# One 64-wide product in place of two 32-wide ones in the 96-row items of a mixture-of-experts kernel

## The reference

```python
def swiglu(x, w13, w2):
    g, u = jnp.split(x @ w13, 2, axis=-1)
    return (jax.nn.silu(g) * u) @ w2

for e in range(N_EXPERTS):          # 8 experts, D_MODEL 1024, D_FF_EXPERT 3584
    out = out + gates[:, e:e + 1] * swiglu(xt, w13[e], w2[e])
```

## Time and profile before

| what | value |
|---|---|
| time, median of 3 runs | 1376.26 us (1376.21 to 1376.49) |
| the profiled execution | 1376.58 us, its span 1374.7 us |
| granted TensorE clock, mean | 0.996 |
| TensorE busy | 1347.6 us, 98% of the span |
| bytes moved by DMA | 444.58 MB |

### The profile page before, as it was taken

The page is one execution under the profiler, slowest core; times in us unless marked ns, Lnnn a source line. Parts: engine busy times, 40 slices in busy tenths (PEclk is TensorE's granted clock), DMA queues, the critical chain, the costliest instruction groups (busy, mean ns, idle before and its releaser), DMA issues.

```text
span 1374.7 us, 29896 instructions
## 1 busy us (share of the span) xinstructions
PE 1347.6 (98%) x13281; PEld 1063.0 (77%) x13281; DVE 411.8 (30%) x761; ACT 321.8 (23%) x587; POOL 13.9 (1%) x27
## 2 busy tenths in 40 slices
PE   9999999999999999999999999999999999999994
PEld 6989888888798888888557888557888557887542
DVE  6677555554747753200100100100100100100102
ACT  6445454443644533000001000001000000000001
POOL 1000000000000000000000000000000000000000
PEclk9999999999999999999999999999999999999998
DMA  8826345555543569999999999999999999999992
GB/s 317 314 96 223 124 169 184 184 187 190 191 154 123 185 250 399 413 378 352 409 421 420 420 419 419 420 421 419 420 420 420 420 421 420 420 420 420 421 420 116
DMA packets 63901, 444.58 MB, mean 323 GB/s; under 512 B 7262, under 2 KB 8686, under 8 KB 10905
## 3 DMA queue, kind: packets, MB, share of 16 engines
q1 hardware_dynamic: 61976, 437.22, 79.7%
q0 software_dynamic: 1792, 5.41, 1.1%
HBM read 441.16 MB, written 1.44 MB: 322 GB/s over the span
## 4 chain that ended last, share of the span: by engine, by line
PE 93%; DVE 3%; DMA 2%; issue 1%; ACT 1%; SPq 0%; DVEq 0%; ACTq 0%
PE bank L1860 52%; PE bank L1440 10%; PE bank L1442 10%; PE bank L1441 10%; PE bank L1824 2%; DMA slot_yT_hi<-in_moe_units 2%; PE bank L1922 2%; PE bank L1834 1%; PE bank L1528 1%; PE bank L1482 1%; PE bank L1835 1%; DVE w_lo L826 1%; PE bank L1649 1%; PE bank L1569 1%; PE bank L1632 1%
## 5 line engine op out<-in xcount | busy, mean ns | idle before, releaser
L1373 DVE TENSOR_TENSOR hidden<-hidden,bank 128x384 f32<-128x384 f32 (+1 forms) x56 | 27.3, 487 | 587.7 <-ACT hidden L786 587.7
L826 DVE TENSOR_TENSOR w_lo<-raw,w_hi 128x1024 fp32r<-128x1024 f32 x154 | 181.1, 1219 | 42.8 <-ACT w_hi L524 41.3
L524 ACT ACTIVATE w_hi<-raw 128x1024 fp32r<-128x1024 f32 x154 | 154.5, 1057 | 40.5 <-PE bank L1442 40.5
L786 ACT ACTIVATE hidden<-bank 128x384 f32<-128x384 f32 (+1 forms) x56 | 24.5, 437 | 365.5 <-PE bank L1860 365.5
L1860 PE MATMUL bank<-raw,mid_x 128*32 128x384 f32 (+1 forms) x1632 | 92.8, 380 | 1.0 <-ACT mid_x L760 1.0
L1860 PEld LDWEIGHTS bank<-raw,mid_x 128*32 128x32 f32 x1632 | 88.7, 110 | 4.5 <-issue 3.1
L779 ACT ACTIVATE hT<-bank 128x384 f32<-128x384 f32 (+1 forms) x56 | 24.5, 437 | 288.5 <-PE bank L1922 288.5
L1440 PE MATMUL bank<-xT_hi,w_hi 128*128 128x256 f32 x320 | 91.8, 287 | 0.0
L1441 PE MATMUL bank<-xT_lo,w_hi 128*128 128x256 f32 x320 | 90.5, 283 | 0.0
L1442 PE MATMUL bank<-xT_hi,w_lo 128*128 128x256 f32 x320 | 90.4, 283 | 0.0
L1440 PE MATMUL bank<-w_hi,xT_hi 128*128 128x512 f32 (+1 forms) x224 | 85.2, 380 | 1.1 <-DVE w_lo L826 0.6
(11 more groups left out here) (326 smaller groups left out, 2100.1 us busy)
## 6 DMA issues: line engine op xcount, KB each, us to landing
raw<-in_moe_units SPq DMA_DIRECT2D x102, 1024.0 KB, 24.9
slot_w_hi<-in_moe_units SPq DMA_DIRECT2D x51, 1024.0 KB, 25.8
slot_w_lo<-in_moe_units SPq DMA_DIRECT2D x51, 1024.0 KB, 26.0
raw<-in_layer_units SPq DMA_DIRECT2D x44, 1024.0 KB, 5.1
raw<-in_dense_units SPq DMA_DIRECT2D x33, 1024.0 KB, 4.9
slot_bias<-in_moe_units SPq DMA_DIRECT2D x17, 1024.0 KB, 26.0
slot_qk<-in_moe_units SPq DMA_DIRECT2D x17, 1024.0 KB, 26.4
slot_memT_lo<-in_moe_units SPq DMA_DIRECT2D x17, 1024.0 KB, 26.7
```

The source lines that it names most:

```text
L524: act.activation(w_hi[:, st.split(u), half, :], raw[:, st.slot(u), half * n:(half + 1) * n], ACT.Copy)\
L786: act.activation(hidden[:, 0:n * P], bank[2][:, 0:n * P], ACT.Silu).then_inc(sem("silu"), 1)
L826: dve.tensor_tensor(w_lo[:, st.split(u), half, :], raw[:, st.slot(u), half * n:(half + 1) * n], w_hi[:, st.split(u), half, :].bitcast(F32) ...
L1373: dve.tensor_tensor(hidden[:, 0:n * P], hidden[:, 0:n * P], bank[j % 2][:, 0:n * P], ALU.mult)\
```

## The change

In the 96-row items tokens 0 to 63 become one product with 64 stationary columns, where they were two products with 32. In `mid_up` that is the case for every k-block, in `mid_down` for blocks 0, 1 and 2, in both banks; block 3 stays as it was. Tokens 64 to 95 (group 2) and everything in group 3 keep 32 columns. The results of each output element are the same sums as before.

```diff
         def mid_up(w, k, b, start, stop):
             a = (k % 4) * 512
-            for g in range(3):
-                r = slice(g * 32, (g + 1) * 32)
+            for r in (slice(0, 64), slice(64, 96)):
                 product(bank[b][r, 0:384], mid_x[:, k, r], w[:, a:a + 384], start, stop)
             for g in range(3):
                 mm = product(bank[b][96:128, g * P:(g + 1) * P], mid_x[:, k, g * 32:(g + 1) * 32], w[:, a + 384:a + 512],
...
             def group(g):
                 return rows[:, block, g * 32:(g + 1) * 32] if block < 3 else rows[:, g, 96:128]
 
-            for g in range(3):
-                product(bank[4][g * 32:(g + 1) * 32, :], group(g), w[:, a:a + 512], start, stop)
+            first_two = ((slice(0, 64), rows[:, block, 0:64]),) if block < 3 else \
+                tuple((slice(g * 32, (g + 1) * 32), group(g)) for g in range(2))
+            for r, held in first_two:
+                product(bank[4][r, :], held, w[:, a:a + 512], start, stop)
+            product(bank[4][64:96, :], group(2), w[:, a:a + 512], start, stop)
             for g in range(2):
                 product(bank[4][96:128, g * 256:(g + 1) * 256], group(g), w[:, a + 768:a + 1024], start and g == 0, stop)
-            for g in range(3):
-                product(bank[5][g * 32:(g + 1) * 32, 0:256], group(g), w[:, a + 512:a + 768], start, stop)
+            for r, held in first_two:
+                product(bank[5][r, 0:256], held, w[:, a + 512:a + 768], start, stop)
+            product(bank[5][64:96, 0:256], group(2), w[:, a + 512:a + 768], start, stop)
             return product(bank[5][96:128, 0:256], group(2), w[:, a + 768:a + 1024], start, stop)
```

## The result

The changed kernel takes 1921.97 us (median of 4 runs, 1921.69 to 1922.43) against 1376.24 us for the kernel before on the same chip: a ratio of 1.3965 (95% interval 1.3941 to 1.399), 545.7 us more. The forecast was 1932 us, in a range of 1760 to 2040.

What follows compares the result with a forecast made beforehand. The prediction took 96-row items as bound by TensorE and 64-row items as living on the weight ring. Adding +410 (k-blocks), +153 (down halves) and -7 (waits) gave +556 us, so 1932 us, range 1760 to 2040.

Steps and rivals of the forecast that it cites:

- part 1: In 96-row items, removing one product per k-block and two per changed down half is worth nothing; the fourth group sets the pace.
- part 2: Inside 96-row items, each change between 64-wide and 32-wide products empties the whole array: 0.095 us, plus an open weight load.
- parts 3 and 4: 96-row items: a k-block takes 1.57 us against 0.655, +410 us; a down half 3.12 against 1.293, +153 us.
- 0.05 + 0.095 and 0.03 + 0.095: Per change in a k-block: open weight load plus emptying of the array, for the 64-wide and the 32-wide phase, in us.
- The sum: Whole kernel: +410 for k-blocks, +153 for down halves, -7 for waits, +556 us in all, giving 1932 us.
- my 616 pairs: Pairs of width changes in four 96-row items: 448 for k-blocks plus 2 x 84 for down halves.
- part 5: Last 64-row item loses its 7.2 us of waits for weights, -7 us; DMA near 170 GB/s in 96-row items.
- Widths side by side: Rival for 96-row items: disjoint columns of different widths run together, time stays 1376 us; chance 0.11.
- A little faster: Rival for 96-row items: fewer instructions let the fourth group run at 0.645 us, 4.5 us less, at most 1372; chance 0.02.
- The clock: Rival for 96-row items: granted clock also drops to 1.2 GHz and streams double, +835, some 2765 us; chance 0.03.

Runs made afterwards that it cites:

- the kernel with one product less: Kernel before, without the up product of rows 32 to 63 in the 96-row items, no width changed: 1375.32 us, ratio 0.9994.
- The kernel without rows 64 to 95: Changed kernel, without the 32-wide up product of rows 64 to 95 in `mid_up`: 1919.56 us.
- the shorter streams: Kernel before, up products of 96-row items with 256 columns instead of 384 and two small products instead of three: 1366.53 us, ratio 0.9927.

## Why the prediction was right, point by point

- **The removed products are worth nothing** (part 1): shown for the up products by the kernel with one product less, 16.27 against 16.28 us a step; for the down products it follows only from the growth of a half, which is the forecast 1.83 us with nothing left over.
- **A change of width empties the whole array, for disjoint columns too** (part 2). In the trace of before that rested on the 0.04 us by which the load at 654.96 waited for the fourth group rather than for its own columns, and on the absence of any change without a stall. The kernel without rows 64 to 95 shows it directly.
- **The price of a k-block and a down half** (parts 3 and 4): predicted 1.57 and 3.12 us. Measured 1.57 and 3.15 from the rounded unit starts, 3.12 from the step with the down products alone changed (1.293 + 5.48 / 3), and 4.4 for blocks 2 and 3 together (3.12 + 1.29 predicted). The price of a pair of changes, 0.05 + 0.095 and 0.03 + 0.095 by my sum, 0.27, was measured as 0.268 and 0.273.
- **The sum.** Predicted +410 and +153, together 563; measured 555.9 in the four items. The term that was too large by 7 us is the number of changes: I gave each 32-wide phase a change behind it, but at the seven transposes of an item, and at its gather, add-backs and border, the width changed before as well. From one matmul record to the next, the 96-row items have 18 or 22 changes before and 316 or 318 after: 1186 more in four items, where my 616 pairs are 1232. The 46 too many, at half of 0.268 us each, are 6.2 of the 7 us. In a step it is 36.23 us against the forecast 36.4.
- **The waits for weights** (part 5): -7 predicted, 87.4 - 80.2 = 7.2 measured. The loads behaved as said, but the rate in the mid items was 180 and 208 GB/s, not 170: I had left out that the ring is filled up again there.
- **What was not in the sum**: the products start 1.0 us earlier (535.66 against 536.7), and the end is 2.5 us shorter. With this, 555.9 - 7.2 - 1.0 - 2.5 = 545.2, the spans differ by 545.3.
- **The rivals.** Widths side by side: not seen. A little faster: the bound of some 10 us that I drew for a faster TensorE is the 9.4 us that the shorter streams gave; with one product less the step did not get faster. The clock: 1.00 in all items.

By the Trainium skill, TensorEngine Tiling (Array Packing), Key Properties, a change of tiling mode drains TensorE. The runs agree: each change between 32 and 64 output columns emptied the array, on disjoint columns too, and a pair of changes cost 0.27 us on top of taking turns.

## What to carry to other kernels

In this kernel (float32, all 128 rows in use, products of 32 and 64 columns) parts of the array ran side by side only while all products had the same width; mixing the two widths made them take turns, and each pair of changes cost another 0.27 us. Other data types and divisions of the rows were not tried. So before merging two narrow products into a wide one, ask what runs beside them and in which width, and which group sets the pace: a product that lies beside a longer group costs nothing, and taking it away gains nothing. A trace that has the operation only at borders can still price it, if one row there separates "waits for its own columns" from "waits for all". And count the changes that were there before.

## What the runs showed of the hardware that I had not expected

After the last item TensorE's sequencer has to run past the six optional items before it may issue the last add-back, and how much of that shows depends on whether TensorE had to wait for weights just before. The chain at the end of the kernel before, and then of the changed one:

```profile
1356.50 0.60 ACT y_hi L769
...
1357.83 5.43 issue
1363.26 0.77 PE bank L1834
```

```profile
1905.53 2.89 issue
1908.42 0.77 PE bank L1834
```

The sequencer's own instructions (marked q) show why: reading the number of items, then the six branches over an item, before and after.

```profile
L1973 PEldq TENSOR_LOAD <-info x1: 487/487/487, 1354.5 to 1354.5; - x1
L1975 PEldq COMPARE_BRANCH  x6: 221/221/3363, 1355.6 to 1362.6; - x6
```

```profile
L1976 PEldq TENSOR_LOAD <-info x1: 484/484/484, 1899.7 to 1899.7; - x1
L1978 PEldq COMPARE_BRANCH  x6: 221/221/3380, 1900.8 to 1907.8; - x6
```

From the reading to the add-back's first product it is 8.7 us in both (1354.53 to 1363.26, 1899.71 to 1908.42; 8.7 to 9.3 in all ten traces), of which the first branch alone takes 3.4. But the changed kernel begins 4.49 us before its last result is read from the bank (1904.20), the kernel before, which was held at its last landing, only 1.97 us (1356.50). All ten traces divide so: 1.96 or 1.97 us and a piece of 5.43 to 6.04 us in the four kernels that wait for their last weights, 4.49 us and 2.87 to 3.42 us in the six that don't. Why the first branch takes 3.4 to 4.0 us and the other five 0.2 was not tried.
